# Centring through six places, squares a product later, and another order of the last tiles in a hybrid decoder layer

## The reference, cut to what matters

```python
z = x @ w_in + b_in                        # 512 x 2048 by 2048 x (7 * 2048 + 16)
glu_val, glu_gate, gate_c, q, k, v, f_logit, gate_a = split_columns(z)
u = glu_val * sigmoid(glu_gate)
c = causal_depthwise_conv(u, w_dw, 31) + b_dw
c = silu(layer_norm(c, g_cn, b_cn))        # the mean and variance over 2048 channels
y_conv = c * silu(gate_c)
y_attn = forgetting_attention(q, k, v, f_logit) * silu(gate_a)     # 16 heads of 128
sub = concat(y_conv, y_attn) @ w_out + b_out                       # 512 x 4096 by 4096 x 2048
out = layer_norm(2 ** 0.25 * x + sub, g_post, b_post)
```

## Time and profile before

| | before |
|---|---|
| median of 3 runs (lowest to highest) | 1600.45 us (1598.1 to 1602.7) |
| the profiled execution: time, span | 1602.69 us, 1600.9 us |
| TensorE busy | 1557.6 us, 97% |
| VectorE busy | 1443.0 us, 90% |
| ScalarE busy | 839.4 us, 52% |
| GpSimd busy | 274.8 us, 17% |
| mean granted TensorE clock | 0.994 |

### The profile page before, as it was taken

The page is one execution under the profiler, slowest core; times in us unless marked ns, Lnnn a source line. Parts: engine busy times, 40 slices in busy tenths (PEclk is TensorE's granted clock), DMA queues, the critical chain, the costliest instruction groups (busy, mean ns, idle before and its releaser), DMA issues.

```text
span 1600.9 us, 29447 instructions
## 1 busy us (share of the span) xinstructions
PE 1557.6 (97%) x11574; PEld 1491.3 (93%) x11574; DVE 1443.0 (90%) x1952; ACT 839.4 (52%) x1224; POOL 274.8 (17%) x295
## 2 busy tenths in 40 slices
PE   7999999999999999999999999999998899999997
PEld 6989999999999999999999999999888888888885
DVE  7669999999999999999999999999967689996787
ACT  5565454554545545455454454554454476744462
POOL 1101112122021121211212212121223200000000
PEclk9999999999999999999999999999999999999998
DMA  8488888999989999899998999998998989887875
GB/s 225 112 199 188 225 203 211 237 210 241 234 204 234 210 249 227 206 238 233 230 221 213 238 232 225 223 222 218 209 276 236 269 296 347 301 232 248 258 213 182
DMA packets 316761, 367.33 MB, mean 229 GB/s; under 512 B 14593, under 2 KB 254369, under 8 KB 315313
## 3 DMA queue, kind: packets, MB, share of 16 engines
q1 hardware_dynamic: 284880, 260.45, 53.1%
q0 software_dynamic: 27360, 100.68, 34.5%
q10 hardware_dynamic: 4384, 4.33, 0.8%
HBM read 286.73 MB, written 87.06 MB: 233 GB/s over the span
## 4 chain that ended last, share of the span: by engine, by line
PE 79%; DVE 9%; DMA 5%; issue 4%; ACT 1%; SPq 1%; POOL 0%; DVEq 0%; ACTq 0%; POOLq 0%
PE ps L1056 26%; PE ps L1057 26%; PE ps L1058 26%; DMA cin<-conv_rows_dram 3%; DVE whl L1308 3%; DVE c_tiles L1409 2%; PE ps L1173 1%; DMA raw<-raw 1%; DVE raw L1327 1%; DMA f_raw<-in_w_in_dram 1%; DMA conv_rows_dram<-c_tiles 1%; DVE raw L1319 1%; SPq L402 1%; DVE xl L1347 0%; ACT whl L781 0%
## 5 line engine op out<-in xcount | busy, mean ns | idle before, releaser
L1056 PE MATMUL ps<-xh,whl 128*128 128x256 f32 x3136 | 897.4, 286 | 22.2 <-DVE whl L1308 10.4
L1057 PE MATMUL ps<-xl,whl 128*128 128x256 f32 x3136 | 889.2, 284 | 0.0
L1058 PE MATMUL ps<-xh,whl 128*128 128x256 f32 x3136 | 889.1, 284 | 0.0
L781 ACT ACTIVATE whl<-raw 128x1024 fp32r<-128x1024 f32 x392 | 415.2, 1062 | 552.7 <-PE ps L1058 441.8
L1056 PEld LDWEIGHTS ps<-xh,whl 128*128 128x128 f32 x3136 | 601.2, 192 | 27.2 <-issue 13.8
L1057 PEld LDWEIGHTS ps<-xl,whl 128*128 128x128 f32 x3136 | 601.6, 192 | 0.5 <-issue 0.5
L1058 PEld LDWEIGHTS ps<-xh,whl 128*128 128x128 f32 x3136 | 601.3, 192 | 0.0
L1308 DVE TENSOR_TENSOR whl<-raw,whl 128x1024 fp32r<-128x1024 f32 x392 | 482.5, 1231 | 61.4 <-ACT whl L781 61.3
L1409 DVE SCALAR_TENSOR_TENSOR c_tiles<-ps,taps,c_tiles 128x511 f32<-128x511 f32 (+14 forms) x480 | 350.6, 730 | 6.8
L630 POOL DMA_DIRECT2D raw<-raw x56 | 49.9, 891 | 483.4 <-DMA raw<-in_w_in_dram 427.3
L1311 DVE TENSOR_TENSOR whl<-raw,whl 128x1024 fp32r<-128x1024 f32 x80 | 97.8, 1223 | 32.4 <-ACT whl L757 32.2
(11 more groups left out here) (185 smaller groups left out, 1552.6 us busy)
## 6 DMA issues: line engine op xcount, KB each, us to landing
raw<-in_w_in_dram SPq DMA_DIRECT2D x224, 512.0 KB, 8.1
raw<-raw POOLq DMA_DIRECT2D x112, 512.0 KB, 6.1
out_sums_dram<-in_w_out_dram POOLq DMA_DIRECT2D x64, 512.0 KB, 9.7
raw<-out_sums_dram SPq DMA_DIRECT2D x64, 512.0 KB, 5.1
raw<-in_w_out_dram SPq DMA_DIRECT2D x48, 512.0 KB, 5.2
out_sums_dram<-in_w_out_dram SPq DMA_DIRECT2D x32, 512.0 KB, 9.4
out_sums_dram<-out_sums_dram SPq DMA_DIRECT2D x32, 512.0 KB, 9.6
x<-in_x_dram SPq DMA_DIRECT2D x8, 512.0 KB, 8.1
```

The costliest lines, as they stand in the source:

```text
L781: nc.scalar.activation(w_high(n), source(n), ACT.Copy).then_inc(high_done, 1)
L1056: nc.tensor.matmul(o, ah, bh, start=start, stop=False, skip_group_check=True)
L1057: nc.tensor.matmul(o, ah, bl, start=False, stop=False, skip_group_check=True)
L1058: return nc.tensor.matmul(o, al, bh, start=False, stop=True, skip_group_check=True)
```

## The change

**Centring.** `CIN` is 6: two more places for tiles lie in `rstd` and `csum`, which are not otherwise used in those groups. `load_cin(j)` from j = 6 on waits for square j - 6 and its store; j = 5 waits for the matmul of the mean, which reads `csum`. The squares stand a slot later: slots 3, 5, 6, and slot 1 of the next group, behind its gates. **Passage.** `load_a(0, 1)` comes after the waits for the stores of the centred tiles, `load_c(0)` behind weight block 4, `load_a(0, 2)` and `(0, 3)` behind blocks 6 and 10. **End.** Tile 0 goes the way of tiles 2 and 3 (ScalarE, GpSimd's DMA, SyncE), with SyncE's writes of it ahead of those of tile 1; VectorE does addition and statistics of a half together, and scales and finishes tile 1 in quarters of 512 columns, with the small steps of the inverse between them; tile 1 is written in four DMAs. **Semaphores.** Some are merged (`s3_s1_s2_done`, `mean_var_done`, `fw_high`), counting the same events; the counts of `cent_stored` and `cin_loaded` follow the six places.

```diff
@@ -47,6 +47,7 @@
 SLOTS = 3
+CIN = 6
 R1, R1_ODD, R2, R5, U_BANK, BANK_A, BANK_B, BANK_C = range(8)
@@ -296,6 +297,10 @@
+        def cin_slot(j):
+            n = j % CIN
+            return cin[:, n, :] if n < 4 else (rstd, csum)[n - 4][:, :]
+
         def z_slot(j):
@@ -404,10 +409,12 @@
             def load_cin(j):
-                if j >= 4:
-                    sp.wait_ge(sq_done, j - 3)
-                    sp.wait_ge(cent_stored[j % 4], 16 * (j // 4))
-                sp.dma_start(cin[:, j % 4, :], conv_dram[j, :, :]).then_inc(cin_loaded[j % 4], 16)
+                if j >= CIN:
+                    sp.wait_ge(sq_done, j - CIN + 1)
+                    sp.wait_ge(cent_stored[j % CIN], 16 * (j // CIN))
+                elif j == CIN - 1:
+                    sp.wait_ge(mean_var_done, 1)
+                sp.dma_start(cin_slot(j), conv_dram[j, :, :]).then_inc(cin_loaded[j % CIN], 16)
@@ -569,25 +576,23 @@
             load_a(0, 0)
-            load_a(0, 1)
             sp.wait_ge(low_done, at(g, 2) + 1)
...
             load_out(3)
-            sp.wait_ge(unit_done, at(g, 2) + 1)
-            load_a(0, 2)
-            for n in range(4):
-                sp.wait_ge(cent_stored[n], 64)
-            sp.wait_ge(unit_done, at(g, 3) + 1)
-            load_c(0)
+            for n in range(CIN):
+                sp.wait_ge(cent_stored[n], 48 if n < 4 else 32)
+            load_a(0, 1)
             sp.wait_ge(low_done, at(g, 4) + 1)
             load_out(4)
-            load_a(0, 3)
+            load_c(0)
             for par in range(2):
...
                 load_out(u)
+                if u in (6, 10):
+                    load_a(0, 2 if u == 6 else 3)
                 if u in (14, 24, 34):
@@ -600,17 +605,16 @@
                         load_z(j)
-            for t in (2, 3):
+            for e, t in enumerate((2, 3, 0)):
                 for h in range(2):
                     c = slice(1024 * h, 1024 * (h + 1))
-                    sp.wait_ge(bpost_added, 16 * (2 * (t - 2) + h + 1))
+                    sp.wait_ge(bpost_added, 16 * (2 * e + h + 1))
                     sp.dma_start(out[0, P * t:P * (t + 1), c], res[t][:, c]).then_inc(stored, 16)
-            for t in range(2):
-                for h in range(2):
-                    c = slice(1024 * h, 1024 * (h + 1))
-                    sp.wait_ge(row_done, 2 * t + h + 1)
-                    sp.dma_start(out[0, P * t:P * (t + 1), c], res[t][:, c]).then_inc(stored, 16)
-            sp.wait_ge(stored, 32 * NT)
+            for n in range(4):
+                c = slice(SEQ * n, SEQ * (n + 1))
+                sp.wait_ge(row_done, n + 1)
+                sp.dma_start(out[0, P:2 * P, c], res[1][:, c]).then_inc(stored, 16)
+            sp.wait_ge(stored, 160)
@@ -729,12 +733,12 @@
             repeat_row(bpost_b[:, :], b_post, bcast_loaded)
-            for t in (2, 3):
+            for e, t in enumerate((2, 3, 0)):
                 for h in range(2):
                     c = slice(1024 * h, 1024 * (h + 1))
-                    if (t, h) != (2, 0):
-                        pool.wait_ge(bpost_added, 16 * (2 * (t - 2) + h))
-                    pool.wait_ge(rows_scaled, 2 * (t - 2) + h + 1)
+                    if e + h:
+                        pool.wait_ge(bpost_added, 16 * (2 * e + h))
+                    pool.wait_ge(rows_scaled, 2 * e + h + 1)
                     repeat_row(res[t][:, c], b_post[c], bpost_added, True)
@@ -927,8 +931,8 @@
                     act.wait_ge(sq_added, j - 1)
-                nc.scalar.dma_start(conv_dram[j, :, :], cin[:, j % 4, :]).then_inc(cent_stored[j % 4], 16)
-                nc.scalar.activation(c_tiles[:, j % 2, :], cin[:, j % 4, :], ACT.Square).then_inc(sq_done, 1)
+                nc.scalar.dma_start(conv_dram[j, :, :], cin_slot(j)).then_inc(cent_stored[j % CIN], 16)
+                nc.scalar.activation(c_tiles[:, j % 2, :], cin_slot(j), ACT.Square).then_inc(sq_done, 1)
@@ -962,19 +966,19 @@
                     if g == HEAD_GROUPS + 2 and s == 6:
-                        act.wait_ge(mean_done, 1)
+                        act.wait_ge(mean_var_done, 1)
                         nc.scalar.activation(mean[:, :], ps[:, BANK_B, :], ACT.Copy).then_inc(mean_read, 1)
-                    if HEAD_GROUPS + 3 <= g < HEAD_GROUPS + 7 and s in (2, 4, 5):
-                        square(4 * (g - HEAD_GROUPS - 3) + (2, 4, 5).index(s))
-                    if HEAD_GROUPS + 3 < g <= HEAD_GROUPS + 7 and s == 0:
+                    if HEAD_GROUPS + 3 <= g < HEAD_GROUPS + 7 and s in (3, 5, 6):
+                        square(4 * (g - HEAD_GROUPS - 3) + (3, 5, 6).index(s))
+                    if HEAD_GROUPS + 3 < g <= HEAD_GROUPS + 7 and s == 1:
                         square(4 * (g - HEAD_GROUPS - 4) + 3)
...
                 if v < 2:
-                    for n in range(4):
-                        act.wait_ge(cent_stored[n], 64)
+                    for n in range(CIN):
+                        act.wait_ge(cent_stored[n], 48 if n < 4 else 32)
                 elif v != E0 // 2:
@@ -1020,12 +1024,12 @@
-            def scale_rows(t):
-                act.wait_ge(fin_vec, INVERSE_AT[t - 2] + 4)
+            def scale_rows(e):
+                act.wait_ge(fin_vec, INVERSE_AT[e] + 4)
                 for h in range(2):
-                    act.wait_ge(scaled_done, 2 * (t - 2) + h + 1)
-                    r = res[t][:, 1024 * h:1024 * (h + 1)]
-                    nc.scalar.activation(r, r, ACT.Copy, scale=rs[:, t - 2:t - 1]).then_inc(rows_scaled, 1)
+                    act.wait_ge(scaled_done, 2 * e + h + 1)
+                    r = res[(2, 3, 0)[e]][:, 1024 * h:1024 * (h + 1)]
+                    nc.scalar.activation(r, r, ACT.Copy, scale=rs[:, e:e + 1]).then_inc(rows_scaled, 1)
@@ -1040,13 +1044,14 @@
                 if u in (93, 96):
-                    scale_rows(2 if u == 93 else 3)
+                    scale_rows(0 if u == 93 else 1)
             for v in range(E0 // 2 + 1, OUT_PAIRS):
...
             deviation(2)
+            scale_rows(2)
             deviation(3)
@@ -1773,24 +1777,48 @@
             dve.wait_ge(bout_added, 32 * NT)
-            for e in (2, 3):
-                t = e - 2
-                for g in range(2):
-                    dve.wait_ge(end_done, 2 * t + g + 1)
-                    add_product(2, t, g, t, 0, ALU.add)
-                dve.wait_ge(c11_read, 2 * t + 2)
-                row_stats(t, 0)
-                dve.wait_ge(stats_done, 12 + 2 * t + 2)
-                moments(e)
-                for h in range(2):
-                    scale_half(e, h)
-                inverse(e)
-                dve.wait_ge(fin_vec, INVERSE_AT[e] + 4)
-                dve.wait_ge(scaled_done, 2 * e + 2)
-                for h in range(2):
-                    c = slice(1024 * h, 1024 * (h + 1))
-                    vec.scalar_tensor_tensor(out=res[t][:, c], in0=res[t][:, c], scalar=rs[:, e:e + 1], in1=bpost_b[:, c],
-                                             op0=ALU.mult, op1=ALU.add).then_inc(row_done, 1)
+            def last_product(t, g):
+                dve.wait_ge(end_done, 2 * t + g + 1)
+                add_product(2, t, g, t, 0, ALU.add)
+                dve.wait_ge(c11_read, 2 * t + g + 1)
+                vec.bn_stats(stats[:, t, g, :], result(t, 0, g)).then_inc(stats_done, 1)
+
+            def scale_quarter(e, n):
+                t, c = (2, 3, 0, 1)[e], slice(SEQ * n, SEQ * (n + 1))
+                vec.scalar_tensor_tensor(out=res[t][:, c], in0=res[t][:, c], scalar=mv[:, 2 * e:2 * e + 1], in1=gpost_b[:, c],
+                                         op0=ALU.subtract, op1=ALU.mult).then_inc(scaled_done, 1)
+
+            last_product(0, 0)
+            last_product(0, 1)
+            dve.wait_ge(stats_done, 14)
+            moments(2)
+            scale_half(2, 0)
+            inverse(2)
+            scale_half(2, 1)
+            last_product(1, 0)
+            last_product(1, 1)
+            dve.wait_ge(stats_done, 16)
+            moments(3)
+            c, base = slice(3, 4), INVERSE_AT[3]
+            scale_quarter(3, 0)
+            scale_quarter(3, 1)
+            dve.wait_ge(fin_act, 4)
+            vec.reciprocal(rs[:, c], std[:, c]).then_inc(fin_vec, 1)
+            scale_quarter(3, 2)
+            dve.wait_ge(fin_vec, base + 1)
+            vec.scalar_tensor_tensor(out=newton[:, c], in0=rs[:, c], scalar=var_eps[:, c], in1=rs[:, c],
+                                     op0=ALU.mult, op1=ALU.mult).then_inc(fin_vec, 1)
+            scale_quarter(3, 3)
+            dve.wait_ge(fin_vec, base + 2)
+            vec.tensor_scalar(newton[:, c], newton[:, c], -0.5, 1.5, ALU.mult, ALU.add).then_inc(fin_vec, 1)
+            dve.wait_ge(fin_vec, base + 3)
+            vec.tensor_tensor(rs[:, c], rs[:, c], newton[:, c], ALU.mult).then_inc(fin_vec, 1)
+            dve.wait_ge(fin_vec, base + 4)
+            dve.wait_ge(scaled_done, 10)
+            for n in range(4):
+                c = slice(SEQ * n, SEQ * (n + 1))
```

(25 more changed lines are left out.)

23 lines of the change are left out of this document (10 added, 13 removed).

## The result

The changed kernel took 1607.07 us (median of 19 runs, 1603.21 to 1611.7) beside 1600.61 us for the kernel before on the same chip (19 runs, 1596.19 to 1606.11): ratio 1.004, 95% interval 1.0029 to 1.0052. It is 6.5 us slower. The forecast was 1606.0, in a range of 1596 to 1612.5.

What follows compares the result with a forecast made beforehand. TensorE was taken as the bound, its gaps in groups 52 to 55 set by cin loads and the fourth square. Centring +4.2 and end +1.3, the rest 0, gave +5.5 on the median 1600.45: 1606.0 us, range 1596 to 1612.5.

Steps and rivals of the forecast that it cites:

- the centring: Groups 52 to 55: six places and later squares together were to cost +4.2 us, bounds 0 and 6.
- the end: After the last matmul: two b_post DMAs of 4.6 us each in a row delay the last writes, +1.3 us.
- Six places: cin loads in the centring: they wait for their turn at SyncE, not for a place, so gain 0.
- Squares a product later: Centring: fourth square at slot 1 makes `sum_3` issue 1.6 to 2.7 us later, taken 2.2; +4.2 us.
- kind A: TensorE gaps ahead of slot 0, waiting for `low` and VectorE for cin; VectorE's 5 to 6 us stalls were to remain.
- kind B: TensorE gaps ahead of slot 5, waiting for `p5` and so `sum_3`; 2.2 us more in each group, all above 3 us.
- Group by group: Slot 5 delays in groups 52 to 55: 0, 0, +3.9, and +4.2 at group 55, the last release counting.
- The passage: Reordered loads: blocks 5 on up to 2.6 us later, covered by ScalarE working three units ahead, so 0.
- The first (cin freed, 1593.5): Rival, centring: two more places free the cin loads, so the kernel gets faster, 1593.5 us; chance 0.15.
- The second (hidden, 1602): Rival, centring: the delay of `sum_3` doesn't reach TensorE, only the end's cost remains, 1602 us; chance 0.26.
- The third (end at +7.5): Rival, end: b_post lands in 7.7 us each, end +7.5 us, total 1612; chance 0.13.
- the fourth (end at -1.7): Rival, end: landings near 3.2 us, so -1.7 us there, total 1603; chance 0.04.

Runs made afterwards that it cites:

- e1: Kernel before with the change's centring alone (six places, squares a slot later, merged semaphores): 1604.82 against 1601.47 us, ratio 1.0019.
- e2: Kernel before with the change's end alone: 1604.41 against 1601.47 us, ratio 1.0015.
- e5: Kernel before with the six places and merged semaphores, squares at their old slots: 1600.57 against 1602.23 us, ratio 0.9994.
- e4_after: The whole changed kernel timed and profiled again, against the kernel before: 1607.13 us, ratio 1.0037.
- e6: Kernel before with GpSimd adding a group's fourth square behind the next group's `sum_3` instead of ahead of it: 1593.1 against 1602.23 us, ratio 0.9953.
- e7: e1 with the same edit of GpSimd's order as e6, against the kernel before: 1594.26 us, ratio 0.9954.
- e11: Kernel before with six places and only the fourth square moved, to slot 1 of the next group: 1606.03 against 1600.36 us, ratio 1.0038.
- GpSimd's turn: The edit of e6, `sum_3` ahead of the fourth square's addition, also in e7, e10 and the whole change; in e6 ratio 0.9953 against the kernel before.
- e3: Kernel before with the change's order of loads at the passage alone: 1602.23 against 1601.47 us, ratio 0.9999.
- e9: e2 with SyncE writing tile 1's quarters ahead of tile 0's second half, against the kernel before: 1603.31 against 1600.36 us, ratio 1.0017.
- e8: Kernel before with a mixed end: tile 0's left half by VectorE, right by ScalarE and one GpSimd DMA, tile 1 by quarters: 1599.37 us, ratio 0.9989.
- e10: Kernel before with the GpSimd order of e6 and the mixed end of e8: 1591.94 against 1600.36 us, ratio 0.9948.

## Why the prediction was right, and where it was not

**The total** was forecast at +5.5 us and measured at +6.5 (1607.07 - 1600.61), and its two terms come out near: the centring +4.2 forecast and +3.3 measured (e1), the end +1.3 and +2.9 (e2). One was a little too large, the other too small by more than half of what it turned out to be. That the total came within 1 us is in part luck: the two errors have opposite signs.

**Six places: 0.** e5 gives -1.0 us within ±2. Right as a price. The reason given, that the loads wait for their turn and not for a place, fits the trace of after: SyncE's turn reads

```profile
1208.92 2.71 SPq L407 DMA_DIRECT2D raw<-in_w_in_dram  x3
...
1211.74 1.92 SPq L417 DMA_DIRECT2D rstd<-conv_rows_dram  x1
```

three blocks, and cin(10) behind them as in the earlier trace rows. SyncE's wait for the store of a tile is gone, as foretold; its waits for a square (line 417 in after) came to 3.5 us in three.

**Squares a product later: `sum_3` 1.6 to 2.7 us later, taken 2.2.** The trace of after has 1188.40, 1214.14, 1238.37 and 1262.09; before had 1185.79, 1212.31, 1237.95 and 1260.14. That is 2.6, 1.8, 0.4 and 2.0 later in absolute time; e4_after gives 3.3, 3.4, 2.3 and 4.0, in an execution that runs later as a whole. From the start of slot 1 it is 1.8 to 2.6 us later in all eight, within the forecast. Against the same group's `low`, the mark that the prediction named, it is 3.2 us (`low` of slot 1), for that `low` now starts sooner. The duration of the addition was forecast between 1.3 and 2.3 and is 2.20. The mechanism is shown by e6, e7 and e11, from both sides: delay that queue more and it costs 5.7 us, take the square out of it and 7.5 us come back (0.47% of 1602). What the gaps ahead of slot 5 would be was wrong: all above 3 us, it said, and one was (4.56, then 2.05, 2.08, 0.93).

**What the prediction had wrong in this part** is what becomes of kind A. It looked for VectorE's stalls of 5 to 6 us to remain, and named their going as a sign that it would be wrong. They went from five with 19.9 us to two with 6.1, and of those for cin(6), (10) and (14) none is left. cin(10) stands behind three weight blocks as before, but SyncE's turn began 2.2 us sooner, with an earlier `low` of slot 0: it was issued at 1211.74 instead of 1214.22, and landed at 1218.0, 6.3 us later, where it took 14.6 in before. In before `sum_3` was issued at 1212.31, ahead of cin(10); in after it is issued at 1214.14, behind it.

Over all traces, those of the experiments too, the order goes with the duration for cin(10) and cin(14): the eight of these loads that were issued 1.9 to 3.3 us ahead of `sum_3` took 6.1 to 7.0 us, the twelve issued 0.8 to 2.5 us behind it 9.7 to 14.6. But it is not the whole cause. cin(6), issued 0.8 to 1.2 us ahead of `sum_3` in four traces, took 10.2 to 13.5 us; and in the four traces with GpSimd's turn, where `sum_3` was issued over 5 us ahead of cin(10) and landed no later than 1.4 us behind its issue, cin(10) still took 11.9 to 12.8. No run separated the two, so the cause stays open. That `sum_3`, issued later, took no longer (7.3 us in group 53 against 8.2) is seen, not explained.

So the later squares have a second effect that pays some of the first back: kind A's two gaps of 4.1 us went, kind B's grew by 3.1. The prediction had counted kind A as swallowed by kind B in groups 52 and 53 and came to nearly the same sum by another way; that, too, is luck.

**Group by group** the sum was 0, 0, +3.9 and +4.2 at slot 5 of group 55. The traces don't show these steps. Slot 0 of group 52 starts at 1178.67 in before and in after; from there after stands at +1.1, -0.6 and +0.6 us at slot 0 of groups 53, 54 and 55 and at -1.5 at slot 5 of group 55, and e4_after, counted likewise, at +1.9, +0.5, +1.9 and +0.5. `sum_3` of group 55 was to go out 4.6 to 5.6 us later and to take 9 us or more; it went 2.0 us later (4.0 in e4_after) and took 7.0 (7.8). The missing ya(1) is not the reason, as e3 shows. One trace can't settle the sum either: that slot starts between 1266.1 and 1272.1 in six traces with the old order of the squares (mean 1269.5) and between 1270.6 and 1274.9 in four with the new one (mean 1272.4). The difference of the means, +2.9, agrees with the timed +3.3; the spread inside each set is larger than it. The half-clock stretches that were forecast behind gaps of over 2 us are not as regular as assumed either: between 1160 and 1300 us they come to 10.24 us both in before and in after, to 13.65 in e4_after and e11, and to 3.41 in e7. In e2 a gap of 2.67 us, ending at 1272.07, has none behind it (granted clock 1.00), and in e6 there is one behind a gap of 1.85 us, ending at 1179.39.

**The passage: 0.** e3 measured 0.9999. Right.

**The end: +1.3 us, measured +2.9 (e2, an interval of -0.2 to +5.0) and, by the traces, 14.76 - 11.35 = +3.4.** The step that failed is the size of one term, the landing of b_post. It was taken at 4.6 us twice; it was 5.06 and 5.87. The issue behind ScalarE, taken at 0.3, came 0.54 us after ScalarE's end (1583.79 to 1584.33). Thus the second landing came 9.3 us behind the last matmul (1595.55 - 1586.2), where 1596.4 - 1589.1 = 7.3 had been forecast. The rest held: the write of 1.5 MB took 5.4 us (5.3 forecast), VectorE's quarters were ready before the second landing (1594.02), and SyncE issued five writes in a row behind it, as foretold. "Here the queue is empty from 1586 on the earlier trace rows, so the low end is nearest" was the false choice: the row of the same line in before had a minimum of 5.5, and that was the nearer row: with 5.5 us for each, the prediction's own sum gives +3.0. The row of line 718, which answers to the earlier trace rows, has in after:

```profile
DMA to landing us min/median/max: 5.1/7.5/9.3
```

The Trainium skill (DMA: Bandwidth & Descriptors, Anatomy of one DMA) makes a DMA of 512 KB by GpSimd an estimate of 3.2 us. The trace doesn't agree for these, which accumulate: 5.06 us with nothing else moving, and 5.87 beside a write of tile 0.

**The rivals.** The first (cin freed, 1593.5) fell as a price: e5 is 1600.57. The mark set for it did come in after, where cin(10) landed at 1218.0 and so ahead of 1222.9, but not through the two places: in e5 it landed at 1225.16. The second (hidden, 1602) fell with e1, whose ratio leaves 1.0 out of its interval, if only just, and more clearly with e11 (1.0026 at least). The third (end at +7.5) and the fourth (end at -1.7) fell with e2 and e9.

## What to carry to other kernels

An in-order engine that issues DMAs makes every instruction ahead of an issue part of that DMA's latency: ask first what stands ahead of a late transfer in its issuer's queue, for here two lines in GpSimd's order were worth 7.5 us and six buffers nothing. At the end of a kernel count the DMAs that stand in a row behind the last operation; splitting a tile into quarters gained nothing here while a slower chain stood ahead of it. Where a change is worth a few tenths of a percent, take its price from timed runs of each part, and from the traces only who waits for whom.

## What the runs showed of the hardware

- **An accumulating DMA at a quiet end is slow, and writes issued behind it are slow too.** 512 KB took 4.9 to 5.2 us in the seven that came first at the end of a trace (in e8 and e10 with a write issued behind it), and 5.6 to 5.9 in the five second ones, which had a write issued just ahead of them. A plain write of 512 KB took 2.6 to 2.7 us, also when it was issued 0.3 us ahead of such a DMA (after); issued 0.9 us behind one it took 5.3 us (e8) and 5.4 (e10). Four writes of 256 KB took 2.1 us each without one (e8) and 4.2 beside one (e9).
- **The same addition on GpSimd takes 1.29 to 2.31 us.** Beside the long ones stand VectorE's products, which then take 1.78 us instead of 0.69. In after it is the same: GpSimd's 2.24 at 1186.21, and VectorE beside it:

```profile
1187.21 1.79 DVE L1542 TENSOR_TENSOR rstd<-rstd,mean 128x512 f32<-128x512 f32 x1
```

- **One load can take twice as long in one trace as in another:** cin(10) took 14.6 us in before, issued 1.9 us behind `sum_3`, and 6.3 in after, issued 2.4 us ahead of it, with the DMA engines 0.89 and 0.91 busy from 1175 to 1275 us.
- **Executions differ by more than most edits here are worth:** slot 5 of group 55 starts within 6 us in six traces with the old order of the squares, three of which (e3, e5, e8) have a gap of 4.0 us on TensorE between 1153 and 1160 us that the other eleven traces lack, and the times of 19 runs of one kernel spread by 8.5 to 10 us.
